# Reading part of one unit's second gather stream beside the next unit's first: 48 v rows of units 0 and 5 move between the u rows of units 1 and 6

## The reference, cut to what matters

```python
q = xb @ w_q                                   # 8 heads, two halves of 128
s1, s2 = scores of each half against 128 sub-keys
best 16 of the 16 x 16 sums of the two top-16 lists   -> idx (128 tokens, 8 heads, 16)
gate = softmax(best_s)
act  = gelu(einsum('td,thkd->thk', xb, u[idx]))
out  = einsum('thk,thkd->td', gate * act, v[idx])
```

## Time and profile before

| | |
|---|---|
| median of 3 runs | 5358.82 us (5356.69 to 5366.58) |
| span of the profiled execution, first to last instruction | 4907.9 us |
| median less span | 450.9 us |
| PE busy | 3090.0 us, 63% |
| DVE busy | 2860.9 us, 58% |
| POOL busy | 2439.9 us, 50% |
| ACT busy | 608.7 us, 12% |
| read from memory | 1604.63 MB, mean 328 GB/s |
| indirect gathers | 2560, 1342.34 MB |
| mean granted PE clock | 0.792 |

### The profile page before, as it was taken

One profiled execution on the slowest core, in us unless ns is written; L12 is line 12 of the kernel. 1 busy time (PEld: TensorE's weight loads), 2 busy tenths in 40 slices (PEclk: granted clock), 3 DMA queues, 4 the chain that ended last, 5 costly groups with the idle time before them and its releaser, 6 DMA issues. The chain is left out here.

```text
span 4907.9 us, 51364 instructions
## 1 busy us (share of the span) xinstructions
PE 3090.0 (63%) x18926; PEld 1914.5 (39%) x18926; DVE 2860.9 (58%) x7102; ACT 608.7 (12%) x1307; POOL 2439.9 (50%) x2565
## 2 busy tenths in 40 slices
PE   6659678721787769656777863682078557558136
PEld 5555643520534554344346353351053333233001
DVE  1339772268336654687687559316934874864850
ACT  2211021200101110111011110210010110110000
POOL 0015255034355435654655754444536766766776
PEclk9679789665797589868988985896579769679679
DMA  6469578277699879999999997797769999999999
GB/s 220 146 201 358 207 260 303 70 266 276 225 413 388 324 299 417 354 401 362 409 367 391 397 385 258 278 342 295 282 202 418 400 395 416 398 401 412 409 420 371
DMA packets 447640, 1611.55 MB, mean 328 GB/s; under 512 B 55328, under 2 KB 57760, under 8 KB 445600
## 3 DMA queue, kind: packets, MB, share of 16 engines
q0 software_dynamic: 368640, 1342.34, 70.7%
q1 hardware_dynamic: 78752, 265.93, 14.6%
HBM read 1604.63 MB, written 3.44 MB: 328 GB/s over the span
## 5 line engine op out<-in xcount | busy, mean ns | idle before, releaser
L643 POOL DMA_INDIRECT ring<-in_peer_u,eidx x1280 | 1207.5, 943 | 1529.2 <-DVE dot L1505 768.5
L643 POOL DMA_INDIRECT ring<-in_peer_v,eidxT x1280 | 1232.1, 963 | 916.2 <-PE acc L930 529.3
L1505 DVE CUSTOM_DVE_ANT_0 ring<-ring,acc 128x1024 f32<-128x1024 f32 x1280 | 1497.2, 1216 | 135.7 <-DMA ring<-in_peer_u,eidx 115.8
L930 PE MATMUL acc<-ring,wz 128*32 128x512 f32 x5120 | 1113.8, 626 | 250.9 <-DMA ring<-in_peer_v,eidxT 238.0
L930 PEld LDWEIGHTS acc<-ring,wz 128*32 128x32 f32 x5120 | 260.6, 112 | 918.7 <-issue 860.3
L883 PE MATMUL pp<-hT,wring 128*128 128x128 f32 x2560 | 330.7, 289 | 47.0 <-DMA wring<-in_w_q 46.6
L685 PE MATMUL tb<-ident,lat 128*128 128x128 f32 (+1 forms) x412 | 101.3, 389 | 405.2 <-DVE lat L1488 390.3
L883 PEld LDWEIGHTS pp<-hT,wring 128*128 128x128 f32 x2560 | 312.6, 202 | 102.7 <-DMA wring<-in_w_q 57.3
L1446 DVE MAX8 v<-lat 128x8 f32<-128x128 f32 x160 | 47.0, 293 | 463.6 <-ACT lat L970 371.6
L727 PE MATMUL pp<-wring,hT 128*128 128x128 f32 (+1 forms) x2240 | 275.4, 286 | 33.4 <-DMA wring<-in_w_in_tail 16.7
L727 PEld LDWEIGHTS pp<-wring,hT 128*128 128x128 f32 x2240 | 269.3, 202 | 49.6 <-DMA wring<-in_w_in 19.9
(11 more groups left out here) (197 smaller groups left out, 3238.5 us busy)
## 6 DMA issues: line engine op xcount, KB each, us to landing
wring<-in_w_q SPq DMA_DIRECT2D x160, 512.0 KB
wring<-in_w_in SPq DMA_DIRECT2D x125, 512.0 KB
wring<-in_w_ada SPq DMA_DIRECT2D x96, 512.0 KB
wring<-in_w_out SPq DMA_DIRECT2D x80, 512.0 KB
ring<-in_peer_u,eidx POOLq DMA_INDIRECT x1280, 6.4
ring<-in_peer_v,eidxT POOLq DMA_INDIRECT x1280, 7.2
wkvb<-in_keys SPq DMA_DIRECT2D x5, 1024.0 KB, 7.0
wqb<-in_wqb SPq DMA_DIRECT2D x4, 1152.0 KB, 11.6
```

What stands on the lines that cost most here:

```text
L643: pool.indirect_dma_start(ring[:, n % GR, :], None, A[table], bass.IndirectOffsetOnAxis(ap=rows, axis=0),).then_inc(s_g[n % GR], 16)
L930: ins = nc.tensor.matmul(acc[32 * q:32 * q + 32, half * 512:(half + 1) * 512], wz[:, at:at + 32], row[:, half * 512:(half + 1) * 512], sta ...
L1505: v.tensor_tensor_reduce(rows, rows, acc[:, :], 1.0, 0.0, ALU.mult, ALU.add, dot[:, n:n + 1])\
```

## The change

It does four things.

- The last 24 v chunks (48 rows) of units 0 and 5 leave their old place and are spread between the u rows of the six 16-row groups in the entry of the next unit: eight v rows in each group of 16 u rows. The other 80 v rows are spread over the old neighbours; for unit 0 also over the attention and the projections of unit 1, which had no rows beside them. A consequence of both is that fewer v rows stand beside each other step.
- Since `acc` still collects v rows of unit 0 or 5 during the entry, `hp` of units 1 and 6 is dropped, and all 128 dots of these two units read the normed rows from `h2` in SBUF.
- `fin` of units 0 and 5 moves behind `soft` of the next unit, in front of its last 32 u rows.
- The waits on counters that counted `hp` are written anew for it; the norm that writes `h2` again two units later waits for the dots.

```diff
+LATE = {0: 24, 5: 24}
...
+def read_late(reads, late):
+
+    return [(step, 2.6 if step[0] == "u" else 0) for step in spread([(r, 1) for r in reads], [(r, 1) for r in late])]
...
-def chosen_and_read(p, t, beside):
+def chosen_and_read(p, t, beside, late):
...
     for hh in range(2, H):
-        out += [(("u", u, c), 2.6) for c in range((hh - 2) * share, (hh - 1) * share)] + [heads[hh]]
+        out += read_late([("u", u, c) for c in range((hh - 2) * share, (hh - 1) * share)],
+                         late[(hh - 2) * len(late) // (H - 2):(hh - 1) * len(late) // (H - 2)]) + [heads[hh]]
...
     for u in range(NU):
-        out += alone(ahead.get(u, []))
         rest = [(("u", u, c), 1) for c in range(NCU)]
+        if u - 1 not in LATE:
+            out.append(("hp", u))
         if u in entry:
-            steps, rest = chosen_and_read(*entry[u])
-            out += [("hp", u)] + steps
-        else:
-            out.append(("hp", u))
+            late = [("v", u - 1, c) for c in range(NCV - LATE.get(u - 1, 0), NCV)]
+            steps, rest = chosen_and_read(*entry[u], late)
+            out += steps
+        if u - 1 in LATE:
+            out.append(("fin", u - 1))
         out += spread(rest, beside_u.get(u, []), dense.get(u, 1.0))
         out.append(("gelu", u))
-        out += spread([(("v", u, c), 1) for c in range(NCV)], beside_v[u], dense.get(u, 1.0))
-        out.append(("fin", u))
+        out += spread([(("v", u, c), 1) for c in range(NCV - LATE.get(u, 0))], beside_v[u] + ahead.get(u + 1, []),
+                      dense.get(u, 1.0))
+        if u not in LATE:
+            out.append(("fin", u))
...
-                    if u >= 2:
-                        act.wait_ge(C["hp"], 2 * (u - 1))
+                    if u - 3 in LATE:
+                        act.wait_ge(C["gu"], H * TOPK * (u - 1))
+                    elif u >= 2:
+                        act.wait_ge(C["hp"], after(("hp", u - 2), "hp"))
...
-                if c == 0:
-                    dve.wait_ge(C["hp"], 2 * (u + 1))
+                normed = h2[:, u % 2, :] if u - 1 in LATE else acc[:, :]
+                if c == 0 and u - 1 in LATE:
+                    p = max(q for q in range(4) if U0[q] <= u)
+                    dve.wait_ge(C["te"], after(("norm", p, u - U0[p], 1), "te"))
+                elif c == 0:
+                    dve.wait_ge(C["hp"], after(("hp", u), "hp"))
...
-                    v.tensor_tensor_reduce(rows, rows, acc[:, :], 1.0, 0.0, ALU.mult, ALU.add, dot[:, n:n + 1])\
+                    v.tensor_tensor_reduce(rows, rows, normed, 1.0, 0.0, ALU.mult, ALU.add, dot[:, n:n + 1])\
```

## The result

The changed kernel takes 5439.23 us (median of 4 runs, 5431.95 to 5450.17) against 5357.75 for the kernel before beside it (4 runs, 5354.89 to 5366.58): a ratio of 1.0151, interval 1.0134 to 1.0168, or +81 us. The forecast was 5415.

The account below looks back on a forecast made before the run. Gathers set the pace on most slices, DVE sets the two entries. Unit 0 -28, unit 5 -41, `fin` +7 and entries +118 gave +56 us: span 4964, with 450.9 around it 5415 us, range 5370 to 5460.

Parts of the forecast that it names:

- unit 0, rest up to `q`: Unit 0 after the scans: 28 v chunks become six before `q`, saving 40 us (-42 to -34).
- unit 5, `topk` ahead of the tail: Behind unit 5's `score`: the first `topk` no longer waits for 11 v chunks and `fin`, -29.3 us.
- two entries: Entries of units 1 and 6: period 27.9 becomes 37.7 us, +59 per entry, +118 together.
- the signs the prediction named: Changed trace: entries 246 us, POOL idle about 5, gathers 1.2 to 1.9, DVE waits; gelu to first `topk` 343 and 223.
- The ring: Entries: ten slots free in order, so POOL stops during `topk`; period 34.8, +41 us per entry; alone 5380 us, chance 0.15.
- The blocking: Entries: gathers starting inside a dot with two SBUF inputs wait for its end; with quicker landings the period is 37.7 us.
- 0.6 of the 14 gathers wait 0.52: Entries, gathers behind gather 11: the average wait beside SBUF dots, priced 14 x 0.31 = +4.4 us a period.
- dots and issues in step: Entries, upper bound: a gather every two dots behind the `topk`, period 41 us, +79 per entry.
- Projections and score: Stage ending in `score`: +12 us at unit 0 (+8 to +17), -7 at unit 5 (-12 to -2).
- 2.0 a run, two of them hidden: Unit 0's projections and score: nine single v chunks come in, two hidden behind the norm, +12 us.
- Behind the entry: `fin` behind `soft`: its gate row stands on PE before the next attention, 3.5 us per unit, +7 (+4 to +14).
- With the 450.9 around it: Whole kernel: 450.9 us taken to lie around the 4907.9 us span, making the forecast span of 4964 a time of 5415.

Follow-up runs that it names:

- the two reruns: Kernel before, unchanged, traced again: 4904.67 us; changed kernel, unchanged, on another chip: 5028.11 against 4907.67 us for the kernel before, ratio 1.0236.
- the blocking taken out: Changed kernel's order, but the 96 dots of each entry read the normed rows from a PSUM bank: 4965.16 against 4910.53 us for before, ratio 1.0112.
- the operand alone: Kernel before with its order kept, but dots of units 1 and 6 read the normed rows in SBUF: 4924.68 against 4910.53 us, ratio 1.0034.
- 18 chunks moved: Changed kernel with PSUM dots, each group's v rows behind its 16 u rows, 18 late chunks: 4881.08 against 4907.67 us for before, ratio 0.9946.
- with 12: Changed kernel with PSUM dots, each group's v rows behind its 16 u rows, 12 late chunks: 4878.08 against 4908.0 us for before, ratio 0.9929.
- with 24 chunks: Changed kernel with PSUM dots, each group's v rows behind its 16 u rows, 24 late chunks: 4895.16 against 4907.67 us for before, ratio 0.9982.

## Why the prediction was right, and where it was not

The direction and both mechanisms of the entry were right; three sizes and one reading were not. The difference between the traces of the two reruns (kernel before to changed kernel, two chips on which before takes 4911 and 4908 us), in us:

| term | predicted | measured |
|---|---|---|
| unit 0, `gelu` to end of scans | -2 | -9.2 |
| unit 0, rest up to `q` | -40 | -35.1 |
| unit 0, attention | +2 | 0 |
| unit 0, projections, `score` | +12 | +27.6 |
| unit 5, `gelu` to `q`, attention | -5 | -2.0 |
| unit 5, projections, `score` | -7 | +3.3 |
| unit 5, `topk` ahead of the tail | -29.3 | -29 |
| two entries | +118 | +149.9 |
| last `topk` to the next `gelu`, both | +7 | +17.8 |
| all else | 0 | +4.9 |
| sum | +56 | +128.2 |

At unit 5 the table splits at the end of ACT's copy, 1.1 us behind `score`, as the prediction does; the stretches above end with `score` itself and give +4.4 for +3.3. Of the signs the prediction named, the stop of POOL and the gathers of 1.2 to 1.9 us are there (3.91 us, 1.68 and 1.99 in the rows above). The entries take 263 and 260 us for 246. From `gelu` to the first `topk` it is 357 and 239 for 343 and 223.

**The ring** was right: 34.8 predicted, 35.4 measured with the blocking taken out, and it moves with the ring's length and with the place of the v rows, as the reasoning by slots in order says.

**The blocking** was the right mechanism with half its price: +2.9 a period predicted, 5.0 measured. The step that was mis-sized is "0.6 of the 14 gathers wait 0.52", 8.4 waits a period and 4.4 us. In the rerun's entry 65 gathers wait, some 11 a period, for 0.64 on average, 6.9 us. Part of the reason is that starts aren't spread by chance. A blocked gather ends 0.81 us behind a dot and the next starts 0.30 later, which in the timeline above is 0.04 us after the next but one dot has begun, so it waits for nearly all of that one too. But this holds for a few gathers behind each stop, not for all: most gathers of an entry take 0.94, and with the operand alone one gets in between two waits even beside dots without a gap (1044.34). So the 40.7 and 40.1 lie close to my upper bound ("dots and issues in step", 41) without being that case. The Trainium skill ("SBUF — State Buffer", the section on the two separate sides) has the rule of the held port pair; the trace agrees, with 1.68 and 1.99 us in the rows above and 0.94 with PSUM dots. The 58 and 120 cycles that the Trainium skill gives as the fixed part from SBUF and from PSUM ("VectorE: DVE Perf Modes", the section on the TRN2 errata) are again not seen as a difference: the changed kernel's dots take 1223 ns from SBUF and 1218 from PSUM.

**Projections and score** were mis-sized, +12 and -7 against +27.6 and +3.3. "2.0 a run, two of them hidden" prices PE's own time alone. PE's waits in that stage of the changed kernel, rerun (time, times, longest):

```profile
PE pp L894 <- DMA wring<-in_w_q: 9.2, 3, 3.7
PE pp L890 <- DMA wring<-in_w_out: 4.2, 1, 4.2
```

and of the kernel before, rerun:

```profile
PE pp L883 <- DMA wring<-in_w_q: 3.0, 7, 0.9
...
PE pp L879 <- DMA wring<-in_w_out: 1.4, 2, 0.8
```

In unit 0's stage seven runs at 2.0 would have been 14, not the 12 of the sum, and the v chunks take 19.8 us of PE. The matmuls of the two projections take 52.6 us for 48.3, at 0.85 for 0.93 of the clock. The waits for weight tiles went from 4.4 to 13.4 us, and PE's other waits fell by some 5 (that for the norm from 5.4 to 3.1). Why the weights come later is not shown. The traffic rose here (217 GB/s for 175), but in unit 5's stage these waits rose too, from 6.8 to 8.3 us, while the traffic fell (272 for 382). There the v chunks take 27.4 us for 25.8 and the projections 49.1 for 48.1, so the fewer rows saved nothing.

**Behind the entry** only `fin` was priced, +3.5 a unit; it is +8.6 and +9.2. The 32 dots left still read SBUF and block: the kernel with the operand alone loses 4 and 5 there. I had given the changed operand no price outside the entries.

**The span.** "With the 450.9 around it" was wrong, and the 5415 came out close partly by luck. On chips where the kernel before takes what its trace shows, the forecast of +56 stands against +120 to +128, about twice as much. On the timed one it is +81. There the changed kernel needs 400 us more than in its rerun, and they all lie in stretches at the pace of gathers: 236 between the `gelu` of units 1 and 5, 131 behind the `gelu` of unit 6, 36 ahead of the first `gelu`; from the `gelu` of unit 0 to that of unit 1 and from 5 to 6 it needs 733.4 + 618.7 us, against 739.4 + 615.4. If all else differs by the 4.9 us of the table there too, the kernel before needed 1352.1 - (81 - 4.9) = 1276 us in these two places, 45 more than the 670.8 + 560.7 of its rerun. It may be its stretches at 308, 276 and 367 GB/s, which the change thinned to 119, 160 and 280; no trace of before from there shows it, so this is argued, not shown.

Open too: why unit 0 takes 374 us from `gelu` to the end of `score` with 18 chunks moved, and 361 with 12, though fewer v rows stand in these stages with 18.

## What to carry to other kernels

In a ring whose slots come free in order, an idle issuer isn't spare room: rows whose consumer never pauses belong behind, not between, the rows whose consumer does, and then they are free up to the issuer's own rate (here a period of 29.6 us for 35.4 with 24 chunks, and of 28.0, nothing added, with 18). Beside gathers that GpSimd issues, it pays to keep one operand of a long VectorE instruction in PSUM (here 5.0 us of a period of 40.4). And where issue and consumption feed each other, starts aren't spread by chance: count the blocked ones in a trace of that operand, for the mean worked out beforehand was too low (4.4 us a period for 6.9).

## What the chip showed beyond that

- A blocked gather waits for the end of the running two-SBUF-input instruction and ends 0.81 us after it, even if the next such instruction has begun already (the gather of 1143.01 ends 0.81 behind the dot that ends at 1143.88, and the next dot had begun at 1143.80). A gather that starts just behind the start of a dot waits for nearly all of it (1144.99: 1.99 us for 0.94), but not each time (1044.34 of the kernel with the operand alone: 0.94).
- The same program took 4908 to 4911 us on three chips, and 5358 where the forecast was timed. In traces of the two kinds, of before and of the changed kernel, the same gathers of units 2 and 3 arrived at 377 and 341 GB/s; why is open. A trace and a time can be from different ones; the execution's own time beside its span tells.
- With the order right, an entry moves 397 GB/s at a DMA share of 0.98, while DVE is busy 95% of it.
